# Starting the second layer's first projection on rows that are not yet normalised, in a two-layer fp32 kernel

## The reference, cut to what matters

```python
    # end of the first layer
    x = x + jnp.square(jax.nn.relu(hm @ w_up[i])) @ w_down[i]
    return rms_norm(x, norm_final)

    # second layer
    ada = (c_act @ w_ada[l] + b_ada[l])[:, None, :]
    shift, scale, gate = jnp.split(ada, 3, axis=-1)
    h = _rms(x, g_pre[l]) * (1.0 + scale) + shift
    proj = h @ w_in[l]
    q, k, v, z_a, u_b, v_b, z_b, g_logits = jnp.split(proj, SPLIT_IDX, axis=-1)
```

## Time and profile before

| | us |
|---|---|
| median of 3 runs | 1375.22 |
| lowest, highest run | 1373.38, 1375.33 |
| the profiled execution's own time | 1371.99 |
| its span (first to last instruction) | 1370.7 |

### The profile page before, as it was taken

The page is one execution under the profiler, slowest core; times in us unless marked ns, Lnnn a source line. Parts: engine busy times, 40 slices in busy tenths (PEclk is TensorE's granted clock), DMA queues, the critical chain, the costliest instruction groups (busy, mean ns, idle before and its releaser), DMA issues.

```text
span 1370.7 us, 20646 instructions
## 1 busy us (share of the span) xinstructions
PE 1344.8 (98%) x8848; PEld 1099.9 (80%) x8848; DVE 823.0 (60%) x1111; ACT 488.2 (36%) x760; POOL 145.3 (11%) x158
## 2 busy tenths in 40 slices
PE   7999999999999999999999999999999999999998
PEld 5587977987888888888788888878887887888886
DVE  7377766846468556574665764555536446786654
ACT  6334154042253343443421322222343234344323
POOL 1022133210010110002110000000130111000000
PEclk9999999999999999999999999999999999999999
DMA  5121011024222333232355542322222433222262
GB/s 191 53 71 47 19 47 63 4 66 166 93 94 91 123 123 109 76 93 92 118 190 194 189 138 92 100 95 94 89 92 76 139 101 114 71 69 70 92 169 93
DMA packets 42524, 137.39 MB, mean 100 GB/s; under 512 B 4777, under 2 KB 8489, under 8 KB 42304
## 3 DMA queue, kind: packets, MB, share of 16 engines
q1 hardware_dynamic: 33984, 114.57, 25.6%
q0 software_dynamic: 4400, 15.90, 3.2%
q10 hardware_dynamic: 4048, 5.59, 1.2%
HBM read 130.27 MB, written 2.10 MB: 97 GB/s over the span
## 4 chain that ended last, share of the span: by engine, by line
PE 88%; DVE 7%; ACT 3%; issue 1%; DMA 1%; POOL 0%; ACTq 0%; DVEq 0%; POOLq 0%
PE bank L464 87%; DVE w_lo L1552 1%; PE bank L467 1%; DVE opA_lo L1560 0%; DVE tmp L1560 0%; ACT L987 0%; DVE GT L1552 0%; DMA xT<-x 0%; DVE BK L1552 0%; ACT scores L987 0%; ACT w_hi L987 0%; ACT exp L987 0%; ACT work L987 0%; DMA w_raw<-panels 0%; DVE AR L1560 0%
## 5 line engine op out<-in xcount | busy, mean ns | idle before, releaser
L1552 DVE TENSOR_TENSOR w_lo<-w_raw,w_hi 128x1024 fp32r<-128x1024 f32 (+1 forms) x209 | 260.2, 1245 | 365.7 <-ACT w_hi L987 365.2
L464 PE MATMUL bank<-opA_hi,w_hi 128*128 128x512 f32 x1000 | 403.8, 404 | 15.2 <-DVE opA_lo L1560 7.8
L464 PE MATMUL bank<-opA_hi,w_lo 128*128 128x512 f32 x1000 | 396.5, 397 | 0.0
L464 PE MATMUL bank<-opA_lo,w_hi 128*128 128x512 f32 x1000 | 395.3, 397 | 0.0
L987 ACT ACTIVATE w_hi<-w_raw 128x1024 fp32r<-128x1024 f32 (+1 forms) x209 | 220.2, 1053 | 373.6 <-DMA w_raw<-panels 367.6
L464 PEld LDWEIGHTS bank<-opA_hi,w_hi 128*128 128x128 f32 x1000 | 188.7, 189 | 68.3 <-issue 17.2
L464 PEld LDWEIGHTS bank<-opA_hi,w_lo 128*128 128x128 f32 x1000 | 188.6, 189 | 45.6
L464 PEld LDWEIGHTS bank<-opA_lo,w_hi 128*128 128x128 f32 x1000 | 188.7, 189 | 44.8 <-issue 1.7
L464 PE MATMUL bank<-opB_hi,w_hi 128*128 128x512 f32 x448 | 178.2, 398 | 0.3 <-DVE w_lo L1552 0.3
L464 PE MATMUL bank<-opB_hi,w_lo 128*128 128x512 f32 x448 | 177.2, 395 | 0.0
L464 PE MATMUL bank<-opB_lo,w_hi 128*128 128x512 f32 x448 | 177.2, 395 | 0.0
(11 more groups left out here) (333 smaller groups left out, 1621.8 us busy)
## 6 DMA issues: line engine op xcount, KB each, us to landing
w_raw<-panels SPq DMA_DIRECT2D x208, 512.0 KB, 3.3
ada_w<-ada POOLq DMA_DIRECT2D x24, 512.0 KB, 4.3
xT<-x ACTq DMA_DIRECT2D x1, 2048.0 KB, 12.0
x_tokens<-x_blocks SPq DMA_DIRECT2D x16, 128.0 KB, 3.9
out<-x_tokens SPq DMA_DIRECT2D x8, 256.0 KB, 2.0
memT<-mem ACTq DMA_DIRECT2D x1, 1024.0 KB, 5.8
rotated_q<-P POOLq DMA_DIRECT2D x4, 256.0 KB, 4.8
xT<-x ACTq DMA_DIRECT2D x3, 256.0 KB, 7.3
```

Of the source, the lines that this page charges most:

```text
L464: return pe.matmul(o, lhsT, rhs, start=start, stop=stop, skip_group_check=True)
L1552: return ve.tensor_tensor(o, a, b, op)
```

## The change

Three things are moved or replaced. The first two qkv panels (`UNSCALED = 2`) are multiplied straight after down3, with rows opB = gain * x that carry neither token factor nor shift; when the factor is known, DVE multiplies the two results by it and POOL adds a shift that is summed with the weights (`shift @ w`). The sums, the root and the spread are put between the steps of these two panels. The next two panels (`AT_ONCE = 2`) are then multiplied in lockstep with the normalised operand, in banks 2 and 3. The unread matmuls go. For `shift @ w` the two panels are loaded a second time, multiplied by the shift and reduced on DVE during down3.

```diff
-         "down1": "hid1", "down2": "hid2", "down3": "hid3", "qkv": "x4", "merge2": "merge2", "out2": "out2"}
+         "down1": "hid1", "down2": "hid2", "down3": "hid3", "qkv": "x3", "merge2": "merge2", "out2": "out2"}
+UNSCALED, AT_ONCE = 2, 2
+F3_SUMS, F3_SPREAD, F3_WEIGHTS = 6, 3, 2
...
+    w_again = [place(f"w_again{n}", [NP, KT, NP], r_p + (6 + 2 * n) * TB) for n in range(UNSCALED)]
+    w_shifted = place("w_times_shift", [NP, KT, NP], r_p + 10 * TB)
+    shift_rows = place("shift_rows", [NP, UNSCALED, NP], r_p + 12 * TB)
+    spread = place("rstd_spread", [NP, S], r_p + 13 * TB)
...
     def bank_of(i):
-        return (0, 1, 6, 7)[i] if i < RW_ALONE else i % 2
+        return (0, 1, 6, 7)[i] if i < RW_ALONE else 2 + i % 2 if at_once(i) else i % 2
...
         def begin(i):
             pe.wait_ge(lo_made, made(i) if i else 1)
-            if i >= RW_ALONE and PANELS[i][0] != "vb":
+            if i >= RW_ALONE and PANELS[i][0] != "vb" and not at_once(i):
                 pe.wait_ge(left[i % 2], left_before(i))
...
(PE)
         p.to("down3")
-        p.steps(KT)
         pe.wait_ge(ada_step, ADA_PARTS)
         for c in range(3 * KT):
             ins = turn(bank[2 + c // 4][:, c % 4 * NP:(c % 4 + 1) * NP], ada_sum[:, c * NP:(c + 1) * NP])
...
         p.to("qkv")
 
-        pe.wait_ge(ada_cols, 7)
-        pe.wait_ge(summed, 3 * KT - 1)
-        token_sums(acc, bank[7], True)
-        pe.wait_ge(summed2, KT - 1)
-        token_sums(acc2, bank[6], True)
-        pe.wait_ge(squared, 5 * KT - 1)
-        last = (FIRST["qkv"] - 1) % 2
-        token_sums(sq[last], bank[7], False)
-        pe.wait_ge(squared, 5 * KT)
-        token_sums(tmp[last], bank[6], False).then_inc(tok_mm, 1)
-        keep_busy(6)
+        pe.wait_ge(ada_cols, 10 + 2 * UNSCALED)
+        for n in range(UNSCALED):
+            mm(bank[4][:, n:n + 1], shift_rows[:, n, :], mat("mean")[:, 0:1])
+        p.steps(F3_SUMS)
+        pe.wait_ge(summed, 3 * KT)
+        token_sums(acc, bank[7])
+        pe.wait_ge(summed2, KT)
+        token_sums(acc2, bank[6]).then_inc(tok_mm, 1)
+        p.steps(F3_SPREAD)
         token_spread(rstd, bank[5], 1)
-        keep_busy(6)
+        p.steps(UNSCALED * KT - F3_SUMS - F3_SPREAD)
...
(ACT)
-            if k == K_HIGH and i + 2 < N_PANELS and not before_heads(i):
+            if k == K_HIGH and i + 2 < N_PANELS and not before_heads(i) and not weights_ahead(i):
                 high(swapped(i + 2))
...
                 act(tmp[j][:, :], xT[:, m, :], ACT.Square, scale=vec("norm_final", m)).then_inc(squared, 1)
+                ac.wait_ge(ada_cols, 10)
+                act(opB[0][:, m, :], xT[:, m, :], ACT.Copy, scale=gain3[:, m:m + 1]).then_inc(op_hi, 1)
...
         token_root(head_cols, 2)
+        high(FIRST["qkv"] + 2)
         for k in range(KT):
             ac.wait_ge(scaled_done, k + 1)
             act(opA[0][:, k, :], tmp[k % 2][:, :], ACT.Identity, bias=adac[:, k:k + 1]).then_inc(op_hi, 1)
+            if k == F3_WEIGHTS:
+                high(FIRST["qkv"] + 3)
+        act(spread[:, :], bank[5][:, :], ACT.Copy).then_inc(heads_hi, 1)
...
(POOL)
-            if name == "down3" and m < KT - 1:
+            if name == "down3":
...
         gp.memset(acc2[:, :], 0.0).then_inc(cleared, 1)
+        gp.wait_ge(ada_step, ADA_PARTS)
+        for n in range(UNSCALED):
+            load(lora_in_s, w_again[n][:, :, :].rearrange("p k n -> p (k n)"), panels[FIRST["qkv"] + n, :, :])
         p.to("ub")
+        gp.wait_ge(ada_cols, 10 + 2 * UNSCALED + 1)
+        for n in range(UNSCALED):
+            i = FIRST["qkv"] + n
+            gp.wait_ge(left[i % 2], left_after(i))
+            gp.tensor_scalar(P[:, Q2 + n, :], hid[i % 2][:, :], q_shift[:, n:n + 1], None, ALU.add).then_inc(cleared, 1)
...
(DVE)
             elif name[:4] == "down":
                 tt(xT[:, m, :], ps, xT[:, m, :], ALU.add).then_inc(left[j], 1)
+                if name == "down3":
+                    ve.wait_ge(left[j], left_after(i))
+                    low_gained(opB, m, xT[:, m, :], gain3[:, m:m + 1], OPERAND["x3"] + m + 1)
+            elif name == "qkv" and m < UNSCALED:
+                ve.wait_ge(heads_hi, parts_after(N_PANELS - 1) + 1)
+                tt(hid[j][:, :], ps, spread[:, :], ALU.mult).then_inc(left[j], 1)
...
         p.to("down3")
-        p.steps(KT)
         for b in range(6):
...
         tt(gain3, gain2, vecs[:, COL["norm_final"]:COL["norm_final"] + 8], ALU.mult).then_inc(ada_cols, 1)
+        p.steps(KT)
+        for n in range(UNSCALED):
+            p.multiply()
+            ve.wait_ge(lora_in_s, 64 + 16 * UNSCALED)
+            if n:
+                ve.wait_ge(ada_cols, 10 + 2 * n)
+            tt(w_shifted[:, :, :], w_again[n][:, :, :], adac[:, 0:KT].unsqueeze(2).broadcast_to([NP, KT, NP]),
+               ALU.mult).then_inc(ada_cols, 1)
+            ve.wait_ge(ada_cols, 10 + 2 * n + 1)
+            ve.reduce_sum(shift_rows[:, n, :], w_shifted[:, :, :].rearrange("p k n -> p n k"), AX.X).then_inc(ada_cols, 1)
+            p.leave()
...
         token_wide(rc, rstd)
+        ts(q_shift, bank[4][:, 0:UNSCALED], float(D), ALU.mult).then_inc(ada_cols, 1)
+        low(FIRST["qkv"] + 2)
         ve.wait_ge(tok_spread, 1)
...
             if k + 2 < KT:
                 scale(k + 2)
+            if k == F3_WEIGHTS:
+                low(FIRST["qkv"] + 3)
         token_wide(r1c, r1)
```

More of the change, by code:

```diff
@@ L104 @@
 OPERAND = {name: 8 * n for n, name in enumerate(
-    ("x", "merge", "mix", "q", "xo", "mlp", "hid0", "hid1", "hid2", "hid3", "x4", "merge2", "out2"))}
+    ("x", "merge", "mix", "q", "xo", "mlp", "hid0", "hid1", "hid2", "hid3", "x3", "x4", "merge2", "out2"))}
 NEEDS = {"rw": "x", "merge": "merge", "mix": "mix", "q": "q", "xo": "xo", "up0": "mlp", "down0": "hid0",
-         "down1": "hid1", "down2": "hid2", "down3": "hid3", "qkv": "x4", "merge2": "merge2", "out2": "out2"}
-CLEAR = {"pad": 2, "mix": 3, "xo": 4, "x3": 5, "x3_gained": 6, "kd": 8}
+         "down1": "hid1", "down2": "hid2", "down3": "hid3", "qkv": "x3", "merge2": "merge2", "out2": "out2"}
+CLEAR = {"pad": 2, "mix": 3, "xo": 4, "x3": 5, "x3_gained": 6, "q_shifted": 8, "kd": 10}
 RW = (12, 13, 14, 0, 4, 8, 1, 5, 9, 2, 6, 10, 3, 7, 11)
@@ L133, in gate_of, with qkv_number, weights_ahead, at_once @@
     return 12 + m if name == "gate" else 3 * (m // 6) + m % 6 - 3
+def qkv_number(i):
+    return i - FIRST["qkv"]
+def weights_ahead(i):
+    return 0 <= qkv_number(i) < UNSCALED
+def at_once(i):
+    return UNSCALED <= qkv_number(i) < UNSCALED + AT_ONCE
+def after_at_once(i):
+    return UNSCALED + AT_ONCE <= qkv_number(i) < UNSCALED + 2 * AT_ONCE
 def before_heads(i):
@@ L289, in build @@
     ada_in = [place(f"ada_w{n}", [NP, D], r_p + (6 + 2 * n) * TB) for n in range(ADA_BUFFERS)]
+    w_again = [place(f"w_again{n}", [NP, KT, NP], r_p + (6 + 2 * n) * TB) for n in range(UNSCALED)]
+    w_shifted = place("w_times_shift", [NP, KT, NP], r_p + 10 * TB)
+    shift_rows = place("shift_rows", [NP, UNSCALED, NP], r_p + 12 * TB)
+    spread = place("rstd_spread", [NP, S], r_p + 13 * TB)
+    q_shift = cols[:, 24:24 + UNSCALED]
     hid = [place(f"hidden{j}", [NP, S], r_p + (24 + j) * TB) for j in range(2)]
@@ L343, in build @@
     vecs_here, mats_here, lora_in_s, x_again, mem_here, ada_rows = (
-        sem("vectors_here"), sem("matrices_here"), sem("lora_here_then_k_swapped"), sem("x_here_again"), sem("mem_here"),
+        sem("vectors_here"), sem("matrices_here"), sem("lora_here_then_w_again_then_k_swapped"), sem("x_here_again"), sem("mem_here"),
         [sem(f"ada_rows{n}") for n in range(2)])
@@ L363, in bank_of @@
     def bank_of(i):
-        return (0, 1, 6, 7)[i] if i < RW_ALONE else i % 2
+        return (0, 1, 6, 7)[i] if i < RW_ALONE else 2 + i % 2 if at_once(i) else i % 2
     def left_before(i):
-        return i // 2 - past_vb(i) if i >= RW_ALONE + 2 else 1
+        return i // 2 - past_vb(i) - after_at_once(i) if i >= RW_ALONE + 2 else 1
     def left_after(i):
@@ L511, in step @@
                 return
-            hi, lo = memo if name == "kv" else opB if name in ("merge", "q", "merge2") or name[:2] == "up" else opA
+            hi, lo = memo if name == "kv" else opB if name in ("merge", "q", "merge2") or name[:2] == "up" or weights_ahead(i) else opA
             n = N_MEM if name == "kv" else S
@@ L526, in mean, with token_sums @@
             mm(bank[7][:, 0:n], mat("mean"), sums[:, 0:n]).then_inc(mean_done, 1)
-        def token_sums(sums, dst, first):
+        def token_sums(sums, dst):
             for q in range(S // NP):
-                ins = mm(dst[:, q:q + 1], sums[:, q * NP:(q + 1) * NP], mat("mean")[:, 0:1], first and q == 0, not first)
+                ins = mm(dst[:, q:q + 1], sums[:, q * NP:(q + 1) * NP], mat("mean")[:, 0:1])
             return ins
@@ L893, in tensor_program @@
         pe.wait_ge(rope_done, 5)
-        pe.wait_ge(lora_in_s, 64 + 32)
+        pe.wait_ge(lora_in_s, 64 + 16 * UNSCALED + 32)
         pe.wait_ge(vt_done, 1)
```

(6 more changed lines are left out.)

1 line of the change is left out of this document (added).

## The result

| | us |
|---|---|
| the changed kernel, median of 18 runs | 1377.51 (1374.98 to 1380.38) |
| the kernel before on the same chip, median of 18 runs | 1374.82 (1372.12 to 1376.46) |
| ratio, 95% interval | 1.0028 [1.0021, 1.0035] |
| the changed kernel's profiled execution, its span | 1375.06, 1373.8 |

The account below looks back on a forecast made before the run. PE, busy 98% of the span, bounds the kernel. With added sums, removed unread matmuls and a new 2.7 us wait, the fifth panel moves from 1054.11 to 1050.4: 3.7 us won, 1371.5 us forecast, own range 1370.8 to 1372.1.

Parts of the forecast that it names:

- DVE in down3: Down3 panels: opB_lo and, in panels 2 and 3, shift product and reduction on DVE, costed at nothing; slip 3.1 us.
- Done about 1026.2: Border behind down3: POOL finishes adding the last tile's squares about 1026.2, in time for the sums at 1026.64.
- The slack of 4.7: Down3: the bank DVE holds is due 4.7 us after its addition ends, so PE does not wait.
- PE's terms: Border: shift sums 0.44, 48 matmuls 11.28, token sums 1.75, spread 0.36, restarts 0.16 us; the pair 11.33.
- The wait before the pair: Before the lockstep panels: PE idles 2.7 us until DVE makes the low part of qkv 3 (w_lo).
- The weights behind the pair: Behind the pair: qkv 5's weights ready at 1055.5 against 1056.1 needed, a margin of 0.6 us.
- the idle 0.49: Between the pair and the next panel: 0.49 us of PE idle time in the kernel before, claimed to go.
- Rival 3: Behind the pair: late weights or banks cost 0.5 to 1 us, leaving 2.7 to 3.2 won; chance 0.11.
- Rival 1: New wait before the pair: the clock falls, costing 1.2 to 1.7 us, leaving 2.0 to 2.5 won; chance 0.17.
- Rival 4: Down3 panels 2 and 3: strided reduction holds a bank; 3.9 us eats the gain, 5.3 gives 1378.0; chance 0.04.
- if PE waits in down3: Sign in PE's timeline of down3: any PE wait there would show the forecast wrong.
- If the reduction takes over 2 us: Sign in DVE's timeline: a shift reduction over 2 us, instead of about 1.25, would show the forecast wrong.

Follow-up runs that it names:

- e5b: The changed kernel with POOL's additions of squares in down3 cut to 8 of 512 tokens; ratio 0.9994 to the kernel before, median 1373.05 us.
- e6b: The changed kernel with the shift product cut to one column and its reduction replaced by zeros; ratio 0.9986 to the kernel before, median 1372.35 us.
- e8: The changed kernel with ada_sum's transposes, their reductions and the shift work moved from down3 into down2's last two panels; ratio 0.9994 to the kernel before.
- e9: e8 with F3_WEIGHTS = 0 instead of 2, so qkv 3's weights are split two tiles earlier; ratio 0.9975 to the kernel before, median 1370.07 us.
- e11: The kernel of e9 measured once more, unchanged; ratio 0.9952 to the kernel before, median 1368.25 us.
- e3: The changed kernel with opB_hi written before the squares on ACT and F3_WEIGHTS = 0 instead of 2; ratio 1.0029 to the kernel before.

## Why the prediction was wrong

**The step that failed** is "DVE in down3", costed at nothing, with its "0.75" for opB_lo. The slip was to be 3.1 us and the wait of PE none. Measured, two panels take DVE 8.83 and 8.69 us (982.99 to 991.82 to 1000.51) against PE's 5.6: a slip of 6.3. The 3.2 between the two are, to 0.1, 2 x 0.7 for the reduction (1.96 against 1.25) and 2 x 0.95 for the room in each panel by which DVE was to recover: opB_lo, longer by 1.1, takes it all. e5b and e6b show both parts: with opB_lo back at 0.75, or without the shift work, the wait for POOL's sums is gone. The slack of 4.7 was right: 6.3 - 4.7 is 1.6, and PE waits 1.59. The forecast also ended its account at PE's bank. A lag that does not hold up PE was taken as free, but xT's addition is the first link of the chain to POOL's sums. "Done about 1026.2" took the squares' start from the earlier trace rows, of the kernel before, where DVE has no lag.

**The price was taken from a row with other neighbours.** 0.75 comes from the earlier trace rows, where POOL does nothing. The trace of before had rows that say more, and I did not read them. DVE's timeline near 193 us, then POOL's:

```profile
192.44 1.18 DVE L1791 COPY work<-cols 128x512 f32<-128x512 f32 x1
193.53 1.77 DVE L1560 SCALAR_TENSOR_TENSOR AR<-work,P_chunk 128x512 f32<-128x512 f32 x1
```

```profile
192.03 1.29 POOL L1377 TENSOR_TENSOR b_scaled<-work,a 128x512 f32<-128x512 f32 x1
193.41 1.35 POOL L1377 TENSOR_TENSOR b_scaled<-b_scaled,work 128x512 f32<-128x512 f32 x1
```

The same kind of instruction on the same shape takes 1.77, and a copy like the earlier trace rows's of 0.43 takes 1.18, both while POOL works. By the Trainium skill, "SBUF — State Buffer", section "SBUF: two separate sides", DVE and GpSimd share one pair of ports; a DVE operation that runs in a two-port mode, or has two inputs in SBUF while a GpSimd operation reads SBUF, and the GpSimd operation take it in turn, each for its whole length. The rows agree for two inputs: opB_lo and w_lo are stretched by 1.0 to 1.2, near the 1.3 of POOL's addition. The copy has one input; whether it ran in such a mode no row shows. xT's addition, with one input in a bank, is 0.68 everywhere, but no row shows it beside POOL.

**Point by point.**
- PE's terms hold: shift sums 0.36, the pair 11.28, passes and matmuls in e8 to within 0.1 us each.
- The wait before the pair: 2.7 forecast, 2.34 measured, 2.43 in e8, released by w_lo as stated.
- The weights behind the pair were in time, and the idle 0.49 went. Rival 3 did not come.
- Rival 1, the clock, came true in another place: behind the token sums, at +1.36 us (forecast 1.2 to 1.7), and not behind the wait before the pair. Its price had been read from the two falls of the kernel before, one of them behind such sums; the place was not foreseen.
- Rival 4, the strided reduction, had the right place and the right direction but a threshold too high. It assumed that DVE recovers 0.95 a panel and that only PE's bank matters. With a recovery of none and the way by POOL included, 1.96 us were enough. Of the two bounds for it, 1.25 and 5.0, the lower was far nearer. Nor does the distance between its elements decide: at 1.25 the two panels would still set DVE back by some 2 x (1.22 + 1.25) = 4.9 us, an estimate from the rows above, and nothing of that is recovered either. No run has the changed kernel with a reduction over neighbours.
- Of the signs named, "if PE waits in down3" came. "If the reduction takes over 2 us" did not, by 0.01 to 0.06: that sign looked at the operation and not at the lag.
- Behind the fifth panel another 0.67 us is lost between the two profiled executions. One wait of 0.28 for ACT (1079.45) is new; the rest was not traced. Other profiles have a longer one at the same panel, up to 1.25, and it differs between executions of one kernel (0.16 in e9, 0.65 in e11).

## What to carry to other kernels

When an engine gets new work that "fits", add up its whole ring, waits included. A lag is only harmless if the ring is shorter than the period of the engine that sets the pace; if it is equal, what is lost once is lost to the end, and the lag must be followed to every consumer and not only to the nearest. Take the duration of a DVE operation from a row in which POOL does what it will do in the new place. And before giving up on a reordering that has come out slower, move its side work to a stage where the engine has room: here that and one constant turned +0.28% into a gain of 0.25% to 0.48%.

## What the hardware showed that I had not expected

**The same idle time is followed by either clock.** In e9 and e11 the kernel is the same. PE idles 2.09 us and starts again near 116.5 us in both. A window of e9, then of e11:

```profile
118.00:120.00 2.00, 2.00 (x10) 1.64 (x9) 1.90 (x3) 0.07 (x1) 0.00 (x0) 1.00 0.00 0
```

```profile
118.00:120.00 2.00, 2.00 (x6) 1.57 (x5) 1.93 (x3) 0.04 (x1) 0.00 (x0) 0.50 0.00 0
```

So an idle time of about 2 us is followed by a fall of the clock in one execution and not in the next. All twelve profiles have this idle time, in the same work; the clock falls behind it in four (e3, e6b, e8, e11). There the stretch from its end to a row that all have near 165 us takes 50.1 to 52.3 us, in the other eight 48.6 to 48.8, so a fall costs 1.5 to 3.7. The same goes for the 2.3 to 2.4 us before the pair: of the six profiles that have it, only e5b's clock falls behind it. Behind the 3.33 us idle at 200 us it falls in all twelve. A forecast should give an idle time of about 2 us a chance of costing 1.5 us or more, not a yes or no, and two profiles should be compared from a point behind such a place. Why it differs between executions stays open.

**Layout costs DVE on either side.** A reduction that reads 1024 elements 512 bytes apart takes 0.76 us more than one that reads neighbours (1.98 against 1.22), and a product that writes 1024 elements 32 bytes apart 1.05 more than one that writes neighbours (2.27 against 1.22).
